# Key pages of a paged cache fetched by keys instead of by heads, in a hybrid decoder step

## The chip, the core and the metric

The kernel runs on one NeuronCore of a Trainium2 chip. Its time is the device time of one execution in microseconds (us). An execution was also taken by the hardware profiler; its trace has the start, length and waits of every instruction, the packets of the DMA engines, and the clock granted to TensorE. Engines are named PE (TensorE), PEld (TensorE's weight loads), DVE (VectorE), ACT (ScalarE), POOL (GpSimd) and SP (SyncE, which issues nearly all DMAs); SPq is SP's own queue of instructions. L724 is line 724 of the kernel.

## The reference, cut to what matters

One inference step of two layers over 256 prompt tokens and 64 sample tokens (8 sequences of 8), all in float32 with a width of 1024. The first layer is a retention layer. The second is block-sparse attention over shared keys and values. Its part that touches the change is the attention of the sample tokens over the paged cache:

```
def per_seq(args):                       # one of the 8 sequences
    q_s, kn, vn, pages = args            # pages: 2 numbers out of 20 physical pages
    k_past = cache_k[pages].reshape(past, MOBA_HEADS, MOBA_HD)      # 256 keys, 8 heads, 128
    v_past = cache_v[pages].reshape(past, MOBA_HEADS, MOBA_HD)
    k_s = concatenate([k_past, kn, zeros])
    v_s = concatenate([v_past, vn, zeros])
    return moba_attend(q_s, q_pos, k_s, v_s, rel_bias)
```

A page is 128 keys by 8 heads by 128 numbers, 512 KB, and lies in HBM key by key (a key's row of all heads is 4 KB). There are 16 pages of keys and 16 of values. `moba_attend` forms the scores of 8 queries against all keys for each head, a softmax with a bias, and the weighted sum of the values.

## The kernel before

All of the work is cut into 52 weight chunks of 1 MB (for each retention head one of q, one of k, two halves of v and two of the gate, then eight of `ro` and four each of `mq`, `mk`, `mv`, `mg`, `mo`). A chunk arrives in one of 3 buffers `w_raw`, ACT splits it into a rounded part `w_hi` (L1229), DVE forms the rest `w_lo` (L1569), each in four parts, into one of 2 buffers; PE then multiplies with `w_hi` and `w_lo` (L927, L930, and L911 for the stacked tile of sample tokens). PE waits for a part of `w_lo` before it uses it.

The order is a list of steps that `make_schedule` writes out by hand; every engine walks this list and does its share of each step, waiting on semaphores. Nothing is reordered at run time: a step that waits on an engine holds up all that stands behind it on that engine. Around the change these steps matter:

- `CHUNK c`: SP issues the load of chunk c + 2 (`load_chunk`, L682), after it has waited until DVE has formed the last parts of chunk c - 1. The chunks called W36 to W40 in the following are number 36 to 40: the four of `mk` (key weights, `in_w_kv`) and the first of `mv`.
- `ME 1` to `ME 6`: SP issues key pages 0 to 5 (`load_page`, L709 to L725).
- `KP n`: DVE waits for page n and turns it (a transpose of 32x32 blocks, L1860), into the layout in which PE's `KS` step multiplies 32 rows of it at a time (L1101). In the same step SP, for n from 1 to 10, issues key page n + 5, after it has waited until page n - 1 has been turned, for its buffer. For n from 13 on it issues value pages.
- `WS c k`: ACT and DVE split part k of chunk c. These stand between the `KP` steps in the same queues.

There are six slots for pages: four in `cache`, and two in the space of `mkT`, which is written later. So SP runs at most six key pages ahead of DVE. The semaphore of a slot counts 64 for a key page, 16 for each of its four DMAs, and `page_count` (L123) adds these up. The page number is read from `pages` into a register (L717) ahead of the DMAs. All of SP's DMAs go into one hardware queue, q1.

In the slot, partition 32 g + i holds keys i, 32 + i, 64 + i and 96 + i of the page, each with the 256 numbers of heads 2 g and 2 g + 1: four runs of 1 KB.

Of the kernel before, what the change touches and what calls it, by code (L numbers as in the profile page):

```python
# [111 lines left out]
def key_page(n):  # L112

    q, s, pg = n // 4, n % 4 // 2, n % 2
    return NPG * (4 * (q // 2) + 2 * s + q % 2) + pg


def page_slot(n):

    return n % NSLOT if n < 2 * NSLOT else (n - 2 * NSLOT) % NCP  # L120
# [191 lines left out]
def build(nc, a):  # L312
# [3 lines left out]
    with ctx:  # L316
# [247 lines left out]
        def page_at(n):  # L564

            at = page_slot(n)
            return cache[:, at, :] if at < NCP else early_pages[:, at - NCP, :]
# [66 lines left out]
        def chunk_source(c):  # L634
            kind, h, i = chunks[c]
            if kind in PAIRED:
                src, off = {"rv": (a["ret_w_in"][0], 2 * RH * DK), "mk": (a["w_kv"], 0), "mv": (a["w_kv"], D),
                            "mo": (a["moba_w_out"][0], 0)}[kind]
                return src.rearrange("(k p) n -> p k n", p=P)[:, KT // 2 * i:KT // 2 * i + KT // 2, off + 512 * h:off + 512 * h + 512]
            if kind[0] == "r" and kind != "ro":  # L640
                col = {"rq": h * DK, "rk": RH * DK + h * DK,
                       "rg": 2 * RH * DK + RH * DV + h * DV + i * 256}[kind]
                return a["ret_w_in"][0].rearrange("(k p) n -> p k n", p=P)[:, :, col:col + 256]
            if kind == "ro":
                return a["ret_w_out"][0].rearrange("(k p) n -> p k n", p=P)[:, KT * h:KT * h + KT, 256 * i:256 * i + 256]
            src, off = {"mq": (a["moba_w_in"][0], 0), "mg": (a["moba_w_in"][0], D)}[kind]
            return src.rearrange("(k p) n -> p k n", p=P)[:, :, off + 256 * h:off + 256 * h + 256]

        def chunk_view(buf, c, s):
            return buf[:, s, :].rearrange("p (k n) -> p k n", k=x_pieces(c))  # L650
# [16 lines left out]
        def _(sp):  # L667
# [41 lines left out]
            def load_page(n):  # L709

                m, vals = (n - 16, True) if n >= 16 else (key_page(n), False)
                before = n - (NCP if n >= 2 * NSLOT + NCP else NSLOT)
                if before >= 16:
                    sp.wait_ge(pv_done, before - 15)
                elif before >= 0:
                    sp.wait_ge(kt_done, before + 1)
                page = sp.value_load(pages[0:1, m:m + 1], min_val=0, max_val=a["cache_k"].shape[0] - 1)  # L717
                if vals:
                    sp.dma_start(page_at(n), a["cache_v"][bass.ds(page, 1)].rearrange("o p h d -> p (o h d)"))\
                        .then_inc(cache_loaded[page_slot(n)], 16)  # L720
                    return
                src = a["cache_k"][bass.ds(page, 1)].rearrange("o (c i) h d -> i (o c) (h d)", i=32)
                for g in range(4):
                    sp.dma_start(page_at(n)[32 * g:32 * g + 32, :].rearrange("p (c x) -> p c x", c=4), src[:, :, 256 * g:256 * g + 256])\  # L724
                        .then_inc(cache_loaded[page_slot(n)], 16)  # L725

            to, src = chunk_view(w_raw, 0, 0), chunk_source(0)
# [17 lines left out]
            for step in steps:  # L745
                kind = step[0]
                if kind == "CHUNK":
                    c = step[1]
# [17 lines left out]
                elif kind == "KT":  # L766
                    h = step[1]
# [7 lines left out]
                elif kind == "SC":  # L775
                    h = step[1]
# [12 lines left out]
                elif kind == "OP":  # L789
                    h = step[1]  # L790
# [23 lines left out]
                elif kind == "ME" and 1 <= step[1] <= NSLOT:  # L814
                    if step[1] == 1:
                        sp.wait_ge(pages_loaded, 16)
                        await_ret_over(sp)
                        sp.dma_start(knw[:, :], bass.AP(a["k_norm_w"].tensor, 0, [[0, P], [1, HD]])).then_inc(knw_loaded, 16)
                    load_page(step[1] - 1)
                elif kind == "KP":  # L820
                    n = step[1]
                    if 1 <= n <= 16 - NSLOT:
                        load_page(n + NSLOT - 1)
                    elif n >= 16 - NCP + 1:
                        load_page(n + NCP - 1)
                elif kind == "SE" and step[1] == 1:
                    await_ks(sp, 3)
                    sp.dma_start(tb[:, :, :], bass.AP(scratch.tensor, FAR - P, [[skew, P], [LINE, MH], [1, TP]]))\
                        .then_inc(tb_loaded, 16)
                elif kind == "KX" and step[1] % 2 == 0:  # L830
                    p = step[1] // 2
                    for n, t in enumerate(tile_order("mk", p, 1)):
                        m = TOK[t][1]
                        sp.wait_ge(rows_done, 3 * p + n + 1)
                        sp.dma_start(k_out[t][:, 512 * p:512 * p + 512], rows[0:m, t, :]).then_inc(rows_stored, 16)
                elif kind == "SN":
                    load_page(16 + NCP - 1)
                elif kind == "PV" and 1 <= step[1] <= 16 - NCP:
                    load_page(15 + NCP + step[1])
                elif kind == "YA" and step[1] == 0:  # L840
                    for t in range(3):
                        await_read(sp, *tile_use("mv", 3 + t))
                    for t, (c0, m) in enumerate(TOK):
                        store(v_out[t], mvp[:, t, :] if t < 2 else mvs[0:TS, :])
                elif kind == "TILE" and chunks[step[1]][0] == "mo":
                    p, t = chunks[step[1]][1], step[2]
                    await_read(sp, *tile_use("mo", 3 * p + t))
                    sp.dma_start(y_out[t][:, 512 * p:512 * p + 512], rows[0:TOK[t][1], t, :]).then_inc(rows_stored, 16)
# [1245 lines left out]
```

## Time and profile before

| | |
|---|---|
| three runs | 506.54, 506.27, 503.84 us; median 506.27 |
| the profiled execution | 503.63 us, of which its span (first to last instruction) is 501.6 us |
| PE busy | 490.5 us, 98% of the span |
| DVE, ACT, POOL busy | 357.9, 261.2 and 97.5 us |
| DMA | 125.54 MB in 86771 packets, 250 GB/s over the span |
| key pages: issues, size, median time to landing | 48 into `cache`, 128 KB, 5.7 us; 16 into `mkT`, 128 KB, 5.5 us |
| value pages | 16, 512 KB, 4.8 us |
| chunks of `in_w_kv` | 8, 1024 KB, 8.7 us |
| granted TensorE clock | 0.999 of full speed in the mean |

A row of a timeline gives the start in us from the start of the span, the length, the engine, the line, the operation, what it writes and reads, a count, and in brackets the idle time of the engine before it and what ended that. A row of stretches gives the length, for each engine its busy time with a count of instructions, the granted clock, the DMA share and the rate. The DMA share is the packets' time over 16 engines' time; it can exceed 1, since packets overlap on an engine. Of a DMA's packets those under 512 bytes in a stretch of large transfers are mostly the writes that report its completion.

### The profile page before, as it was taken

The numbers are of one execution on the slowest core, as the hardware profiler recorded it, in microseconds if no ns is written. First come the engines' busy times: TensorE is split into PE (matmuls) and PEld (weight loads), VectorE is DVE, ScalarE is ACT, GpSimd is POOL, SyncE is SP. The second block draws the span as 40 slices with busy tenths as digits, with TensorE's granted clock in tenths as the row PEclk, the third lists the DMA queues.
The fourth block names the chain that finished last, engine by engine and source line by source line (L and its number), as shares of the span: only waits on it lengthen the run. The fifth ranks groups of instructions, "written<-read, shape, count | busy, mean of one in ns | idle before, by whom it ended". The sixth has DMA issues, their size and how long they took to land.

```text
span 501.6 us, 9903 instructions
## 1 busy us (share of the span) xinstructions
PE 490.5 (98%) x3689; PEld 423.9 (85%) x3689; DVE 357.9 (71%) x633; ACT 261.2 (52%) x536; POOL 97.5 (19%) x139
## 2 busy tenths in 40 slices
PE   8999999999999999999999999999799999999997
PEld 6989978899778987799799999987567878999885
DVE  3955539884799819895589978996865764776662
ACT  6735532564427715366454455853637655655630
POOL 0291003620073200920000052454002000000000
PEclk9999999999999999999999999999999999999999
DMA  9993979999899898999936979979998567683211
GB/s 264 350 344 113 273 252 304 383 364 230 280 338 392 245 225 307 352 348 255 257 131 219 345 237 276 230 172 200 256 316 262 186 205 236 232 309 135 85 52 52
DMA packets 86771, 125.54 MB, mean 250 GB/s; under 512 B 5492, under 2 KB 51525, under 8 KB 86597
## 3 DMA queue, kind: packets, MB, share of 16 engines
q1 hardware_dynamic: 85874, 124.63, 80.7%
q8 instruction: 29, 0.48, 0.4%
q0 software_dynamic: 768, 0.28, 0.4%
q14 instruction: 18, 0.14, 0.1%
q10 hardware_dynamic: 82, 0.02, 0.0%
HBM read 98.93 MB, written 27.57 MB: 252 GB/s over the span
## 4 chain that ended last, share of the span: by engine, by line
PE 90%; DMA 3%; DVE 2%; ACT 2%; issue 2%; SPq 1%; POOL 0%; DVEq 0%; ACTq 0%; POOLq 0%
PE bank L930 46%; PE bank L927 17%; PE bank L911 7%; PE bank L1039 3%; DMA w_raw<-in_w_kv 2%; PE bank L1159 2%; PE bank L1053 1%; PE bank L986 1%; SPq L724 1%; PE bank L1205 1%; PE bank L1019 1%; PE bank L1021 1%; PE bank L1020 1%; PE bank L1007 1%; PE bank L1192 1%
## 5 line engine op out<-in xcount | busy, mean ns | idle before, releaser
L1569 DVE TENSOR_TENSOR w_lo<-w_raw,w_hi 128x512 fp32r<-128x512 f32 x207 | 143.2, 731 | 65.8 <-ACT w_hi L1229 65.0
L1229 ACT ACTIVATE w_hi<-w_raw 128x512 fp32r<-128x512 f32 x208 | 118.6, 620 | 71.6 <-PE bank L930 35.7
L930 PE MATMUL bank<-xn_hi,w_hi 128*128 128x320 f32 x320 | 100.2, 317 | 0.8 <-ACT w_hi L1229 0.7
L930 PE MATMUL bank<-xn_hi,w_lo 128*128 128x320 f32 x320 | 97.7, 309 | 0.1
L930 PE MATMUL bank<-xn_lo,w_hi 128*128 128x320 f32 x320 | 97.6, 309 | 0.0
L927 PE MATMUL bank<-w_hi,xn_hi 128*128 128x512 f32 x160 | 64.8, 405 | 0.0
L930 PEld LDWEIGHTS bank<-xn_hi,w_hi 128*128 128x128 f32 x320 | 59.7, 188 | 5.0 <-issue 2.9
L927 PE MATMUL bank<-w_lo,xn_hi 128*128 128x512 f32 x160 | 62.5, 391 | 0.0
L927 PE MATMUL bank<-w_hi,xn_lo 128*128 128x512 f32 x160 | 62.5, 390 | 0.0
L930 PE MATMUL bank<-ym_hi,w_hi 128*128 128x320 f32 x192 | 60.9, 317 | 0.0
L930 PEld LDWEIGHTS bank<-xn_lo,w_hi 128*128 128x128 f32 x320 | 59.8, 188 | 0.4 <-DVE xn_lo L1618 0.2
L930 PEld LDWEIGHTS bank<-xn_hi,w_lo 128*128 128x128 f32 x320 | 59.7, 188 | 0.3 <-DVE w_lo L1569 0.3
L930 PE MATMUL bank<-ym_hi,w_lo 128*128 128x320 f32 x192 | 59.3, 309 | 0.0
L930 PE MATMUL bank<-ym_lo,w_hi 128*128 128x320 f32 x192 | 59.3, 309 | 0.0
L1788 DVE SCALAR_TENSOR_TENSOR st<-st,bank 128x512 f32<-128x512 f32 x64 | 39.7, 684 | 5.2 <-PE bank L1053 5.2
L1997 POOL TENSOR_TENSOR fin<-raw_qk,cst 128x320 f32<-128x320 f32 x16 | 17.3, 1101 | 109.3 <-DMA out_ret_state_prompt<-fin 101.7
L930 PEld LDWEIGHTS bank<-ym_hi,w_hi 128*128 128x128 f32 x192 | 36.1, 188 | 1.8 <-issue 1.7
L927 PEld LDWEIGHTS bank<-w_hi,xn_hi 128*128 128x128 f32 x160 | 30.0, 188 | 8.6 <-issue 3.1
L930 PEld LDWEIGHTS bank<-ym_lo,w_hi 128*128 128x128 f32 x192 | 36.1, 188 | 0.1
L930 PEld LDWEIGHTS bank<-ym_hi,w_lo 128*128 128x128 f32 x192 | 36.0, 188 | 0.0
L927 PEld LDWEIGHTS bank<-w_lo,xn_hi 128*128 128x128 f32 x160 | 30.1, 188 | 6.6
L927 PEld LDWEIGHTS bank<-w_hi,xn_lo 128*128 128x128 f32 x160 | 30.1, 188 | 5.5
(289 smaller groups left out, 783.6 us busy)
## 6 DMA issues: line engine op xcount, KB each, us to landing
w_raw<-in_ret_w_in SPq DMA_DIRECT2D x23, 1024.0 KB, 11.3
st<-in_state_ret SPq DMA_DIRECT2D x32, 512.0 KB, 8.6
out_ret_state_sample<-st SPq DMA_DIRECT2D x32, 512.0 KB, 4.5
w_raw<-in_ret_w_out SPq DMA_DIRECT2D x8, 1024.0 KB, 8.5
w_raw<-in_moba_w_in SPq DMA_DIRECT2D x8, 1024.0 KB, 6.5
w_raw<-in_w_kv SPq DMA_DIRECT2D x8, 1024.0 KB, 8.7
cache<-in_cache_v SPq DMA_DIRECT2D x16, 512.0 KB, 4.8
cache<-in_cache_k SPq DMA_DIRECT2D x48, 128.0 KB, 5.7
```

The costliest lines, as they stand in the source:

```text
L724: sp.dma_start(page_at(n)[32 * g:32 * g + 32, :].rearrange("p (c x) -> p c x", c=4), src[:, :, 256 * g:256 * g + 256])\
L911: mm = pe.matmul(bank[b][:, :], xn_hi[:, k, TP:T + TS], w[:, wk, :], start=k == 0 and n == 0, stop=k == KT - 1 and n == 1)
L927: mm = pe.matmul(bank[b][0:m, :], x[:, k, c0:c0 + m], w[:, wk, :], **flags)
L930: mm = pe.matmul(bank[out][:, 0:T], w[:, wk, P * tile:P * tile + P], x[:, k, :], **flags)
L986: mm = pe.matmul(bank[5][0:m, col:col + n], kT[:, d, j:j + m], qT[:, d, i0:i0 + n], start=d == 0, stop=d == 1)
L1007: mm = pe.matmul(o[:, P:TP], vp[:, 1, at], sT_own[:, :], start=False, stop=True)
L1039: mm = pe.matmul(bank[5][32 * j:32 * j + 32, :], qz[:, q0:q0 + 32], st[:, b, DV * d:DV * d + DV], start=False, stop=g == 1 and d == 1, ski ...
L1159: mm = pe.matmul(bank[7][32 * j:32 * j + 32, P * u:P * u + P], window(8 * half_at + 4 * (j // 2) + 2 * pg + j % 2, b % 4), page_at(16 + m) ...
L1229: act.activation(w_hi[:, c % 2, part], w_raw[:, c % RAW, part], ACT.Copy).then_inc(w_hi_done, 1)
L1569: dve.tensor_tensor(w_lo[:, c % 2, part], w_raw[:, c % RAW, part], w_hi[:, c % 2, part].bitcast(F32), ALU.subtract).then_inc(w_lo_done, 1)
L1788: dve.scalar_tensor_tensor(state, state, math.exp(NEW * LOG_DECAY[h]), bank[up_bank(b, d)][:, :], ALU.mult, ALU.add).then_inc(bank_read[up ...
L1997: done(pool.tensor_tensor(to, x, tab, ALU.mult))
```

## The change

The key page is still fetched with four DMAs of 128 KB, of 128 runs of 1 KB each, and every run ends in the same place. Before, DMA g fetched heads 2 g and 2 g + 1 of all 128 keys into the 32 partitions from 32 g on. Now DMA c fetches keys 32 c to 32 c + 31 with all heads, into 1 KB of each of the 128 partitions.

```
-                src = a["cache_k"][bass.ds(page, 1)].rearrange("o (c i) h d -> i (o c) (h d)", i=32)
-                for g in range(4):
-                    sp.dma_start(page_at(n)[32 * g:32 * g + 32, :].rearrange("p (c x) -> p c x", c=4), src[:, :, 256 * g:256 * g + 256])\
+                src = a["cache_k"][bass.ds(page, 1)].rearrange("o (c i) h d -> (o c) i (h d)", i=32)
+                for c in range(4):
+                    sp.dma_start(page_at(n)[:, 256 * c:256 * c + 256], src[c].rearrange("i (g x) -> g i x", g=4))\
                         .then_inc(cache_loaded[page_slot(n)], 16)
```

The DMA's two sides, outermost first, as counts:

| | destination (SBUF) | source (HBM) |
|---|---|---|
| before | 32 partitions, 4 runs, 256 numbers | 32 keys (4 KB apart), 4 groups of keys (128 KB apart), 256 numbers |
| after | 128 partitions, 1 run, 256 numbers | 4 pairs of heads (1 KB apart), 32 keys (4 KB apart), 256 numbers |

On SP, around the load of W39 (the rows are the last two DMAs of page 12, the chunk, and the beginning of page 13; ISA rows set registers), before:

```order
L724 DMA cache<-in_cache_k 32x4x256
L724 ISA
L724 DMA cache<-in_cache_k 32x4x256
L682 DMA w_raw<-in_w_kv 128x4x512
L717 TENSOR_LOAD pages
L717 ISA x2
L724 ISA
L724 DMA cache<-in_cache_k 32x4x256
```

The same rows now:

```order
L724 DMA cache<-in_cache_k 128x1x256
L724 ISA
L724 DMA cache<-in_cache_k 128x1x256
L682 DMA w_raw<-in_w_kv 128x4x512
L717 TENSOR_LOAD pages
L717 ISA x2
L724 ISA
L724 DMA cache<-in_cache_k 128x1x256
```

No row has moved; only the shape of the destination differs, in all 64 DMAs of key pages. PE, DVE, ACT and POOL have the same rows as before.

## Rows read from the trace of the kernel before

**Rows 1.** The page's chain that ended last: shares of the span by engine.
```profile
PE 90%; DMA 3%; DVE 2%; ACT 2%; issue 2%; SPq 1%; POOL 0%; DVEq 0%; ACTq 0%; POOLq 0%
```

**Rows 2.** SP's timeline: start us, length us, line, transfer, how many.
```profile
301.71 4.47 SPq L724 DMA_DIRECT2D cache<-in_cache_k  x8
306.63 0.40 SPq L682 DMA_DIRECT2D w_raw<-in_w_kv  x1
...
316.25 0.40 SPq L682 DMA_DIRECT2D w_raw<-in_w_kv  x1
...
328.61 1.82 SPq L724 DMA_DIRECT2D cache<-in_cache_k  x4
330.53 0.40 SPq L682 DMA_DIRECT2D w_raw<-in_w_kv  x1
331.69 8.34 SPq L724 DMA_DIRECT2D cache<-in_cache_k  x12
340.81 5.28 SPq L724 DMA_DIRECT2D mkT<-in_cache_k  x8
346.86 2.18 SPq L724 DMA_DIRECT2D cache<-in_cache_k  x4
349.15 0.40 SPq L682 DMA_DIRECT2D w_raw<-in_w_kv  x1
350.31 8.33 SPq L724 DMA_DIRECT2D cache<-in_cache_k  x12
358.74 0.40 SPq L682 DMA_DIRECT2D w_raw<-in_w_kv  x1
```

**Rows 3.** Stretches, with TensorE's idle time; columns are named in the first row.
```profile
core 0: us, PE busy (x) PEld busy (x) DVE busy (x) ACT busy (x) POOL busy (x), PEclk, DMA share, GB/s
...
352.00:370.00 18.00, 13.52 (x177) 9.32 (x176) 14.54 (x23) 8.51 (x23) 0.00 (x0) 1.00 1.08 280
370.00:400.00 30.00, 29.33 (x312) 22.80 (x311) 19.65 (x43) 19.80 (x49) 2.88 (x5) 1.00 0.75 251
```

**Rows 4.** ACT's timeline, splits of W39 and W40; in brackets idle before.
```profile
360.74 1.67 ACT L1229 ACTIVATE w_hi<-w_raw 128x512 fp32r<-128x512 f32 x3 [1.61 <-DMA w_raw<-in_w_kv]
...
369.29 1.16 ACT L1229 ACTIVATE w_hi<-w_raw 128x512 fp32r<-128x512 f32 x2 [4.76 <-DMA w_raw<-in_w_kv]
372.21 0.59 ACT L1216 ACTIVATE rows<-bank 64x512 f32<-64x512 f32 x1 [1.77 <-PE bank L911]
```

**Rows 5.** DVE's timeline: turning of pages 6, 7 and 15.
```profile
339.01 1.25 DVE L1860 STREAM_TRANSPOSE mvp<-cache 128x1024 f32<-128x1024 f32 x1
343.24 1.25 DVE L1860 STREAM_TRANSPOSE mvp<-cache 128x1024 f32<-128x1024 f32 x1 [2.98 <-DMA cache<-in_cache_k]
...
367.20 1.23 DVE L1860 STREAM_TRANSPOSE mvp<-cache 128x1024 f32<-128x1024 f32 x1
```

**Rows 6.** Stretches, columns as in rows 3: v_rows, weights, key pages.
```profile
46.00:47.00 1.00, 1.00 (x9) 1.00 (x8) 0.00 (x0) 0.97 (x3) 0.23 (x1) 1.00 0.53 199
302.00:304.00 2.00, 2.00 (x16) 2.00 (x15) 1.84 (x5) 2.00 (x5) 0.28 (x1) 1.00 1.09 380
304.60:310.00 5.40, 5.40 (x39) 5.40 (x38) 5.37 (x8) 1.47 (x5) 0.00 (x0) 1.00 1.13 219
```

**Rows 7.** DMA packets from 302 to 304 us, then 304.6 to 310.
```profile
DMA packets 761, 0.76 MB, mean 380 GB/s; under 512 B 6, under 2 KB 761, under 8 KB 761
...
DMA packets 1147, 1.18 MB, mean 219 GB/s; under 512 B 123, under 2 KB 1025, under 8 KB 1146
```

**Rows 8.** DMA from 45 to 48.6 us, all v_rows; GB/s in 40 slices.
```profile
GB/s 0 0 0 137 68 114 68 137 91 68 159 182 205 182 205 182 228 182 182 205 228 228 182 182 137 137 137 182 159 205 228 205 182 159 250 182 137 68 46 0
DMA packets 288, 0.52 MB, mean 146 GB/s; under 512 B 32, under 2 KB 32, under 8 KB 288
```

**Rows 9.** SP's DMAs: ns min/median/max, first and last start.
```profile
L772 SPq DMA_DIRECT2D v_rows<-vs_split x16: 570/573/692, 44.0 to 223.7; - x16
...
L724 SPq DMA_DIRECT2D cache<-in_cache_k x48: 316/318/1445, 301.7 to 358.3; - x48
```

## The prediction

> **What bounds the kernel now.** I read the chain that ended last first: TensorE holds 90% of the span [rows 1], so a change pays or costs only where it makes TensorE wait. Then the key pages. SP fetches sixteen of them, each with four DMAs of 128 KB, between 301.7 and 358.7 us, with weight chunks W36 to W40 (the w_kv rows) in the same in-order queue [rows 2] (the eight DMAs of pages 2 and 3, and of 4 and 5, stand between these rows). In that stretch the DMA engines are the bound: from 352 to 370 us their busy share is 1.08, and TensorE is busy for 13.52 us of 18, so 4.48 us are missing there; in the 30 us behind it only 0.67 are [rows 3]. The ACT rows say who is late: the split of W39 waited 1.61 us and that of W40 4.76 us for the DMA [rows 4]. On VectorE the turning of page 7 waited 2.98 us for its page, and the last page is turned at 367.20 us [rows 5]. So pages and weight chunks compete for the same DMA engines, and TensorE feels it a little already.
>
> The same views price the traffic. Ahead of the pages the last weights for q (1 KB packets to 128 partitions) run at 380 GB/s. Behind them the pages of before (1 KB packets, 32 partitions each) run at only 219 GB/s, at a full share of 1.13 [rows 6]. Each of the 16 engines moves about 24 GB/s in the first case and 13.7 in the second. The packet size is no reason for it, since 302 to 304 us is nearly all 1 KB packets (761 under 2 KB, 0.76 MB) [rows 7]; the narrow destination is what differs.
>
> **The change, step by step.** On SP the same 64 DMAs stand in the same places; on the other engines nothing changes. Each still has 128 runs of 1 KB. What changes is the pair of shapes: 32 partitions on both sides before; now 128 partitions on the destination, but a source that says 4 groups of heads, then 32 keys, then 256 numbers. The outermost counts no longer agree: 128 and 4.
>
> (1) How many engines carry it. The trace has one kind of DMA with outermost counts that disagree: v_rows, 64 partitions on the one side, 8 on the other (8x8x512 in the code: sequences, tokens, values). Four of them move 0.52 MB in 256 packets, and beside these stand exactly 32 small completion packets: 8 for each DMA [rows 8]. For the key pages, 32 and 32, the small packets are 123 beside 1.17 MB, which is 9 DMAs: 13.8 each, 16 with the window's edges cut [rows 7]. In its steady part v_rows reaches a share of 0.53 [rows 6]. So a DMA of 8 and 64 used 8 engines, and I read a DMA of 4 and 128 as using 4. The Trainium skill ("DMA: Bandwidth & Descriptors", section on why a DMA increments its semaphore by 16) says it as a rule: the number of engines is the largest up to 16 that divides both sides' slowest size that isn't 1, and on SP's queue they are the lowest-numbered ones. By that rule it is 4, and always the same four; the completion packets of v_rows agree with the first half, and no row here shows the second. Without the skill it is an assumption of mine that every page goes to the same four; if they rotated, the load would be as even as before (in rival B).
>
> (2) What one page then takes. v_rows moved 199 GB/s on 8 engines, 25 each [rows 6]; in the full stretches an engine does 24. Bounds for an engine that takes keys: 13.7 GB/s (the page rows of before) and 28 (228 GB/s on 8, which v_rows' small slices reach again and again [rows 8]). I take 24, for each of the four now writes to partitions of its own, and the narrow destination shared by 16 engines is gone. A page is 512 KB, 131 KB for each of 4 engines: 5.46 us. A weight chunk still goes over all 16, 65.5 KB each: 2.73 us, and it lands only when its share on the four busy engines has.
>
> (3) The queue. The four engines are free at 304.6 us, when the traffic ahead of the pages ends [rows 6]. In SP's order they get pages 0, 1, W36, 2, 3, W37, 4, 5, 6, W38, 7 to 12, W39, 13 to 15, W40. One after the other:
> - page 6 is in at 304.6 + 7 x 5.46 + 2 x 2.73 = 348.3 (turned at 339.0 now);
> - page 7 at 304.6 + 8 x 5.46 + 3 x 2.73 = 356.5 (343.24 now);
> - W39 at 304.6 + 13 x 5.46 + 4 x 2.73 = 386.5 (split begins at 360.74 now);
> - page 15 at 304.6 + 16 x 5.46 + 4 x 2.73 = 402.9 (turned at 367.20 now);
> - W40 at 405.6 (split begins at 369.29 now).
> SP never starves them: it may run 6 pages ahead of VectorE, 33 us of work at this pace. VectorE waits at each page with the w_lo splits behind it, and TensorE waits for those; that is how late pages reach it.
>
> (4) The end. W40 is 405.6 - 369.3 = 36.3 us late, page 15 35.7. Everything behind them is as it was, but for the 1.77 us that ACT now waits for TensorE behind W40's first split [rows 4], which is gone when TensorE has been standing for long: 34.5. The 4.48 us that TensorE loses before 370 are inside this difference of two times already.
>
> (5) SP's issue. A v_rows DMA holds SP for 573 ns, a key DMA for 318 [rows 9]. If the unequal shapes are the cause, 0.25 us for each DMA and 1.0 for a page: SP then needs about 3 us a page against 5.46 on the engines. Cost 0; the queue on the four engines hides it. If that cover were gone (16 engines), it would be seen, see below.
>
> (6) TensorE's clock. It is granted in full (1.00) through 352 to 370 us [rows 3], with 4.48 us idle in several pieces. With gaps of up to 5 us at each page it may fall to half for a while. Inside the starved stretch this costs nothing; behind it a few matmuls at most. Between 0 and 4 us, I take 0.5.
>
> Sum: 34.5 + 0.5 = +35 on the profiled execution, 503.63 us, whose span is 501.6: 538.6. The median of the runs, 506.27, lies 2.64 above that execution, so I say 541.3.
>
> **Rivals.**
> - A, the other side: all 16 engines take part. Then the wide destination brings pages to the rate of rows to 128 partitions, 380 against 219 GB/s, 1.4 us a page in place of 2.4; W39 and W40 come in time, and TensorE gets back its 4.48 us between 352 and 370. 499.1 for the profiled execution, 501.8 in the runs. It decides if completion packets are 64 a page. For it: the rates [rows 6], and that the destination is 128 partitions. The Trainium skill ("SBUF — State Buffer", the section on the DMA port swizzle) has the same rule, that partitions 0 to 31 reach 8 of 16 ports; the ratio 219 to 380 is near it. Against it: the 8 packets of v_rows, whose 64 partitions did not help. Chance 0.06.
> - B: 16 engines, but SP pays 0.25 us more for each DMA. W39 is issued behind 24 key DMAs in a row, +6 us; W40 behind 36, +9, at 367.9; at 380 GB/s it lands 3.5 us later, 2 us behind now. Chance 0.04, 508. Here I put also 8 engines, or four that rotate, at 25 GB/s each: about the 219 of now. Another 0.05, 504 to 510.
> - C: the four engines disturb each other. Engines on partitions 0 to 31 and 32 to 63 walk in step, and if these share a port (the same section of the skill says that bit 5 of the partition doesn't change the port) both may fall to the 13.7 of the page rows. A page is then 9.6 us: 304.6 + 16 x 9.6 + 5 x 2.73 = 471.9, 102.6 us late, 606 for the profiled execution. With the engines partly out of step it ends between. v_rows, whose shares also lie 32 partitions apart, showed no such loss. Chance 0.13, from 560 to 610.
>
> **How the numbers follow.** Forecast 0.72, at 541. Its own range comes from the rate: 28 GB/s gives 304.6 + 16 x 4.68 + 5 x 2.34 = 391.2, +20 after the 1.77, 526; 20 GB/s gives 6.55 and 3.28, 425.8, +54.7, 561. The range should reach a little into C: 522 to 580. Left out are A and B and most of C, near 0.2. Within 0.5% of 506.27 (about what the runs can tell from no change) lies most of B: 0.05. Faster: A and a rest of B, 0.06. Slower 0.89.
>
> **What would show it.** Right: in the stretch from 305 to about 400 us a DMA share near 0.3 and 100 GB/s; 16 small packets to a page in place of 64; key DMAs without a landing time, as the v_rows have none, or with one of tens of us; long waits of VectorE at L1860 for the cache DMA; the splits of W39 and W40 waiting for DMA; TensorE with gaps in 340 to 405, and all as before behind it. Step 2 is wrong if the share is near 0.3 but the rate under 80 GB/s. Step 1 is wrong if the share stays at 1 or the small packets at 64. Step 4 is wrong if the stretch behind W40 is longer or shorter than the 132 us of now. Step 5 shows in the ns of L724's DMAs.

## The result, and the profile after

The changed kernel takes 555.8 us in the median of 4 runs, against 505.3 us before: a ratio of 1.0995, with a 95% interval of 1.095 to 1.104. It is 10% slower. The profiled execution took 556.13 us, of which its span is 554.1 us. Ratios here and below compare undisturbed executions alone; two of the twelve of experiment 9 were disturbed, and they stand in its median but not in its ratio.

The stretch of the key pages is where it went. First the stretches of the changed kernel, with the columns of [rows 3], in order of time: the last weights for q ahead of the pages, a stretch in which TensorE starves, a page stretch with nothing beside it, a stretch around the last pages, and all that comes behind the split of W40.

```profile
core 0: us, PE busy (x) PEld busy (x) DVE busy (x) ACT busy (x) POOL busy (x), PEclk, DMA share, GB/s
302.00:304.00 2.00, 2.00 (x16) 2.00 (x15) 1.83 (x6) 2.00 (x5) 0.44 (x2) 1.00 1.08 383
360.00:370.00 10.00, 2.38 (x81) 1.58 (x92) 2.42 (x3) 1.74 (x3) 0.00 (x0) 0.50 0.28 91
372.20:389.80 17.60, 8.53 (x29) 6.21 (x29) 8.36 (x12) 5.88 (x15) 0.00 (x0) 0.81 0.27 89
410.00:420.00 10.00, 6.04 (x68) 4.42 (x80) 3.06 (x3) 0.00 (x0) 0.00 (x0) 0.83 0.93 291
420.34:554.10 133.76, 124.34 (x1031) 105.50 (x1012) 79.71 (x182) 69.53 (x171) 2.73 (x5) 0.98 0.51 176
```

From 372.2 to 389.8 us the DMA engines are used to 0.27 of sixteen, which is 4.3 engines, and move 89 GB/s; in [rows 6] the pages of before had a share of 1.13 and 219 GB/s. The weights ahead of the pages run at 383 GB/s, as before. TensorE is busy for 2.38 us of 10 between 360 and 370 us, and for 6.04 between 410 and 420. Behind W40 the stretch is 133.8 us long, against 132.3 in [rows 3, 4] (501.6 - 369.3).

The packets of that page stretch, the counterpart of [rows 7]:

```profile
DMA packets 1568, 1.57 MB, mean 89 GB/s; under 512 B 48, under 2 KB 1566, under 8 KB 1566
```

1.57 MB are 12 DMAs of 128 KB, three pages, in 17.6 us: 5.87 us each. Beside them stand 48 completion packets, 4 for a DMA, where the pages of before had about 14 to 16 and v_rows 8 [rows 8]. Per engine it is 22.3 GB/s.

ACT's splits that wait for a chunk, VectorE's turning of the pages that answer to [rows 5], and the ns of SP's DMAs that answer to [rows 9]:

```profile
337.96 1.15 ACT L1229 ACTIVATE w_hi<-w_raw 128x512 fp32r<-128x512 f32 x2 [8.46 <-DMA w_raw<-in_w_kv]
...
360.51 1.15 ACT L1229 ACTIVATE w_hi<-w_raw 128x512 fp32r<-128x512 f32 x2 [15.27 <-DMA w_raw<-in_w_kv]
...
399.27 1.67 ACT L1229 ACTIVATE w_hi<-w_raw 128x512 fp32r<-128x512 f32 x3 [5.52 <-DMA w_raw<-in_w_kv]
...
420.34 1.15 ACT L1229 ACTIVATE w_hi<-w_raw 128x512 fp32r<-128x512 f32 x2 [16.77 <-DMA w_raw<-in_w_kv]
```

```profile
343.78 1.25 DVE L1860 STREAM_TRANSPOSE tb<-mkT 128x1024 f32<-128x1024 f32 x1 [1.01 <-DMA mkT<-in_cache_k]
350.15 1.25 DVE L1860 STREAM_TRANSPOSE tb<-mkT 128x1024 f32<-128x1024 f32 x1 [4.55 <-DMA mkT<-in_cache_k]
...
366.32 1.25 DVE L1860 STREAM_TRANSPOSE mvp<-cache 128x1024 f32<-128x1024 f32 x1 [7.35 <-DMA cache<-in_cache_k]
...
372.19 1.25 DVE L1860 STREAM_TRANSPOSE ktc<-cache 128x1024 f32<-128x1024 f32 x1 [3.46 <-DMA cache<-in_cache_k]
...
378.07 1.25 DVE L1860 STREAM_TRANSPOSE ktc<-cache 128x1024 f32<-128x1024 f32 x1 [1.10 <-DMA cache<-in_cache_k]
...
389.81 1.25 DVE L1860 STREAM_TRANSPOSE scr<-mkT 128x1024 f32<-128x1024 f32 x1 [4.06 <-DMA mkT<-in_cache_k]
...
410.82 1.25 DVE L1860 STREAM_TRANSPOSE mvp<-cache 128x1024 f32<-128x1024 f32 x1 [4.06 <-DMA cache<-in_cache_k]
417.77 1.25 DVE L1860 STREAM_TRANSPOSE mvp<-cache 128x1024 f32<-128x1024 f32 x1 [5.13 <-DMA cache<-in_cache_k]
```

```profile
L724 SPq DMA_DIRECT2D cache<-in_cache_k x48: 537/1204/2236, 301.9 to 408.1; - x48
```

The splits are those of W37, W38, W39 and W40; the pages are 4, 5, 7, 8, 9, 11, 14 and 15. W39 is split 38.5 us later than in [rows 4] (399.27 against 360.74), W40 51.05 us later; page 7 is turned at 366.32 in place of 343.24, the last page at 417.77 in place of 367.20. Pages 7, 8 and 9 come 5.87 us apart, and page 11 twice that behind page 9. A key DMA holds SP for 1204 ns in the median, where it was 318.

### The profile page after: what moved, and what is told of

Its sections match the earlier page's. It is cut to its first block, busy times and chain, and to the rows that moved or that the text cites. A ratio compares the mean times of both kernels' runs of the same rounds, so it can differ in the third digit from the quotient of the medians.

```text
span 554.1 us, 9903 instructions
## 1 busy us (share of the span) xinstructions
PE 502.1 (91%) x3689; PEld 431.0 (78%) x3689; DVE 358.7 (65%) x633; ACT 260.8 (47%) x536; POOL 97.1 (18%) x139
## 4 chain that ended last, share of the span: by engine, by line
PE 74%; SPq 12%; DVE 5%; issue 4%; DMA 3%; ACT 2%; POOL 0%; DVEq 0%; ACTq 0%; POOLq 0%
PE bank L930 36%; PE bank L927 15%; SPq L724 9%; PE bank L911 5%; PE bank L1039 3%; SPq L717 2%; DVE w_lo L1569 2%; PE bank L1159 1%; DMA out_k_prompt<-rows 1%; PE bank L1053 1%; PE bank L986 1%; DMA cache<-in_cache_k 1%; PE bank L1205 1%; SPq L682 1%; ACT w_hi L1229 1%
## 5 line engine op out<-in xcount | busy, mean ns | idle before, releaser
L927 PE MATMUL bank<-w_hi,xn_hi 128*128 128x512 f32 x160 | 67.4, 421 | 3.9 <-DVE small L1737 2.0
L927 PE MATMUL bank<-w_lo,xn_hi 128*128 128x512 f32 x160 | 64.6, 404 | 0.0
L927 PE MATMUL bank<-w_hi,xn_lo 128*128 128x512 f32 x160 | 64.5, 403 | 0.0
L911 PE MATMUL bank<-w_hi,xn_hi 128*128 128x512 f32 x80 | 33.8, 423 | 11.7 <-DVE w_lo L1569 10.6
L927 PEld LDWEIGHTS bank<-w_hi,xn_hi 128*128 128x128 f32 x160 | 31.4, 196 | 14.3 <-issue 3.6
L927 PEld LDWEIGHTS bank<-w_lo,xn_hi 128*128 128x128 f32 x160 | 31.3, 196 | 7.2
L927 PEld LDWEIGHTS bank<-w_hi,xn_lo 128*128 128x128 f32 x160 | 31.5, 197 | 5.9
```

The costliest lines, as they stand in the source:

```text
L911: mm = pe.matmul(bank[b][:, :], xn_hi[:, k, TP:T + TS], w[:, wk, :], start=k == 0 and n == 0, stop=k == KT - 1 and n == 1)
L927: mm = pe.matmul(bank[b][0:m, :], x[:, k, c0:c0 + m], w[:, wk, :], **flags)
```

## The experiments

The kernel before was run again beside each; its medians lay between 505.6 and 506.4 us.

**1. Is it the number of engines, or the pieces of 1 KB to 128 partitions?** The same four DMAs, with a source that also counts 128 outermost:

```
-                src = a["cache_k"][bass.ds(page, 1)].rearrange("o (c i) h d -> (o c) i (h d)", i=32)
+                src = a["cache_k"][bass.ds(page, 1)].rearrange("o p h d -> p (o h d)")
-                    sp.dma_start(page_at(n)[:, 256 * c:256 * c + 256], src[c].rearrange("i (g x) -> g i x", g=4))\
+                    sp.dma_start(page_at(n)[:, 256 * c:256 * c + 256], src[:, 256 * c:256 * c + 256])\
```

> The changed kernel's four DMAs a page, 1 KB pieces to all 128 partitions, but read from rows of the page as they lie, so that both sides count 128 outermost (a partition then holds another key and other heads than it should; the sum of work is the same). Theory (the outermost counts 4 and 128 put a page on four engines): 64 completion packets a page, a page in under 2 us, a rate above 330 GB/s, no wait for W39 and W40, 498 to 503 us. Rival (pieces of 1 KB to 128 partitions are slow whatever the source): share and rate as in the changed kernel, about 556 us.

Measured: 501.3 us, ratio to before 0.990 (0.987 to 0.994). The stretches of this kernel that answer to [rows 3, 6], and the packets from 304.6 to 310 us:

```profile
304.60:310.00 5.40, 5.40 (x39) 5.40 (x39) 5.29 (x8) 1.47 (x5) 0.00 (x0) 1.00 0.90 272
312.00:317.00 5.00, 5.00 (x36) 5.00 (x35) 4.78 (x11) 3.73 (x9) 2.18 (x6) 1.00 0.51 161
352.00:370.00 18.00, 16.07 (x191) 12.01 (x190) 14.27 (x21) 8.43 (x21) 0.00 (x0) 1.00 0.91 305
...
DMA packets 1268, 1.47 MB, mean 272 GB/s; under 512 B 119, under 2 KB 988, under 8 KB 1267
```

The whole loss is gone, and 1% is gained on before. Of the 988 packets under 2 KB 119 are small, which leaves 869 of 1 KB, 6.8 key DMAs; the rest are 2 KB packets of W36. 119 small ones beside 6.8 key DMAs and a part of W36 fit 16 for each DMA, and not 4. The rate was below what I expected (272 GB/s, then 161 and 305). With a share of 0.51 from 312 to 317 us the engines are waiting for work, as SP's rows show:

```profile
307.70 5.74 SPq L724 DMA_DIRECT2D cache<-in_cache_k  x8
316.16 0.40 SPq L682 DMA_DIRECT2D w_raw<-in_w_kv  x1
```

Eight DMAs, 1.05 MB, take SP 5.74 us, which is 183 GB/s, and then it issues nothing for 2.7 us, until W37's buffer is free. ACT still waits 4.07 us for W40, which I had expected to be gone. So the destination and the size of the pieces are innocent; what costs is that the two sides' outermost counts differ. This source also reads 1 KB of each key, where the changed kernel reads 32 keys as they lie one behind the other. Nor is that the cause: the value pages are read as they lie too, with 128 partitions against 128 keys, and their 512 KB landed 4.8 us after the issue in the kernel before, less than the 5.87 us that four engines need for as much.

**2. Two engines in place of four.** Everything lands where it should (and `page_count` adds 128 for a key page in place of 64):

```
-                for c in range(4):
-                    sp.dma_start(page_at(n)[:, 256 * c:256 * c + 256], src[c].rearrange("i (g x) -> g i x", g=4))\
+                for half in range(2):
+                    for c in range(4):
+                        sp.dma_start(page_at(n)[64 * half:64 * half + 64, 256 * c:256 * c + 256],
+                                     src[c][:, 512 * half:512 * half + 512].rearrange("i (g x) -> g i x", g=2))\
```

> A page in eight DMAs of 64 KB, each to 64 partitions from 2 pairs of heads x 32 keys: outermost counts 2 and 64, everything lands where it should. Theory (engines = what divides both counts, here 2): 2 completion packets a DMA, share near 0.14, 45 GB/s, a page 262144/22.3 GB/s = 11.75 us; W40 at 304.6 + 16 x 11.75 + 5 x 4.4 = 514.6 in place of 420.3, about 650 us. Rival (SP's 1.2 us for each such DMA is the cost): 8 x 1.3 = 10.4 us a page only if SP is slow by itself, 628; rival (any unequal shape costs the same): 556.

Measured: 648.3 us, ratio 1.280 (1.271 to 1.289). A stretch of pages alone, and its packets:

```profile
430.00:450.00 20.00, 1.11 (x3) 0.33 (x1) 4.25 (x6) 2.63 (x8) 0.00 (x0) 0.50 0.14 45
...
DMA packets 886, 0.89 MB, mean 45 GB/s; under 512 B 27, under 2 KB 884, under 8 KB 884
```

Share 0.14, 45 GB/s, and 27 small packets beside 0.88 MB, which is 13.5 DMAs of 64 KB: 2 each. W40's split begins at 514.11 us where the queue of pages gave 514.6. The time follows the count of engines: 16, 4 and 2 give about 501, 556 and 648 us.

**3. Is SP's longer issue the bound?** One DMA a page, still 4 against 128, with the keys permuted (`page_count` adds 16):

```
-                src = a["cache_k"][bass.ds(page, 1)].rearrange("o (c i) h d -> (o c) i (h d)", i=32)
-                for c in range(4):
-                    sp.dma_start(page_at(n)[:, 256 * c:256 * c + 256], src[c].rearrange("i (g x) -> g i x", g=4))\
+                src = a["cache_k"][bass.ds(page, 1)].rearrange("o (i g) h d -> (o g) i (h d)", g=4)
+                sp.dma_start(page_at(n), src)\
```

> One DMA of 512 KB a page, outermost counts 4 and 128, runs of 4 KB (keys 4 i + g in the place of 32 g + i, so the keys are permuted). Theory (four engines are the bound, and SP's 1.2 us a DMA is only that it is held back by them): a page still takes 5.4 to 5.9 us, 548 to 557 us. Rival (SP's issue of 1.2 us a DMA is the bound, 4 to a page): a page 1.3 us of SP, 505 to 515 us.

Measured: 551.0 us, ratio 1.087 (1.080 to 1.093). A quarter of the DMAs saves 5 us of 50. The page's DMA now holds SP for up to 6.2 us:

```profile
L723 SPq DMA_DIRECT2D cache<-in_cache_k x12: 628/2758/6244, 303.2 to 389.2; - x12
```

So SP is held back by work already queued on the engines, and most of its time for an issue is a result. The changed kernel says the same by itself: its first six key DMAs take SP 0.54 to 0.73 us, near the 0.57 of v_rows, and the next two 1.06 and 2.07. In experiment 1, with equal counts, the median is 0.33. Runs of 4 KB go at 102 GB/s on four engines (the pages turned at 364.32 and 369.42 us are 5.1 us apart), runs of 1 KB at 89.

**4. Only the first six pages in the new form.**

```
+                if n < 6:
+                    (the changed kernel's four DMAs)
+                    return
                 (the four DMAs of the kernel before)
```

> Key pages 0 to 5 in the new form, 6 to 15 in the form of before. Theory (one queue on four engines, to be worked off in order): page 5 is in at 304.6 + 6 x 5.87 + 2 x 4.4 = 348.6 against 337.6 when it is turned in the kernel before, then pages at 2.4 us each catch up nothing: W40 some 12 us later than 369.3, 514 to 518 us. Rival (every page costs its 50/16 us): 524. Rival (the first six are fetched far ahead, so they are hidden): 505 to 508.

Measured: 528.5 us, ratio 1.043 (1.036 to 1.050). All three expectations missed: 514 to 518, 524 and 505 to 508. It is no case of "fetched ahead, therefore hidden": six pages of sixteen cost 23 us of the 50.

```profile
345.48 1.25 DVE L1866 STREAM_TRANSPOSE tb<-mkT 128x1024 f32<-128x1024 f32 x1 [1.00 <-DMA mkT<-in_cache_k]
355.30 1.25 DVE L1866 STREAM_TRANSPOSE tb<-mkT 128x1024 f32<-128x1024 f32 x1 [8.00 <-DMA mkT<-in_cache_k]
...
364.33 1.15 ACT L1235 ACTIVATE w_hi<-w_raw 128x512 fp32r<-128x512 f32 x2 [18.05 <-DMA w_raw<-in_w_kv]
...
393.55 1.15 ACT L1235 ACTIVATE w_hi<-w_raw 128x512 fp32r<-128x512 f32 x2 [5.72 <-DMA w_raw<-in_w_kv]
```

W40's split begins at 393.55, 24.3 us late, where I had 12. The 12 was a wrong comparison: I set page 5's arrival, 348.6, against 337.6, when the kernel before turns that page. It had been in its slot for 11 us by then; its DMAs there were issued by 321.5 us and landed within 5.2:

```profile
L724 SPq DMA_DIRECT2D mkT<-in_cache_k x8: 316/317/325, 317.4 to 321.5; - x8
...
DMA to landing us min/median/max: 4.8/5.0/5.2
```

In the kernel before the queue behind page 5 goes on at 328.61 [rows 2]; by my sum it does so at 348.6 here, 20.0 us later, which gives 505.7 + 20 = 525.7 against the 528.5 measured. Of the other 4.3 us of W40's delay the rows tell where they begin: page 5 is turned at 355.30, 6.7 us later than the 348.6, and 9.82 us behind page 4, where it was 6.37 in the changed kernel (343.78 and 350.15). Up to page 5 the queue on the four engines is the same in both. What differs is the twelve others, which here have pages 6 and later and W38 to fetch: the DMA share in that interval is 0.98, against 0.39. So the four carried page 5 at 13.3 GB/s each while the twelve were busy. By what the twelve slow them isn't shown.

**5. Is it the order in the queue or the bytes on the four engines?** W36 to W40 issued by ACT, on a queue of its own:

```
+                elif kind == "CHUNK" and 36 <= step[1] + 2 <= 40:
+                    c = step[1] + 2
+                    await_lo(act, c - RAW, 2)
+                    await_lo(act, c - RAW, 3)
+                    act.dma_start(chunk_view(w_raw, c, c % RAW), chunk_source(c)).then_inc(w_loaded[c % RAW], 16)
```

> The changed kernel with the loads of W36 to W40 issued by ACT, at the same step, on its own queue. Theory (the bytes of pages and chunks on the four engines set the pace, whatever the order): W39 and W40 come earlier, page 15 is still turned near 415 to 418 us, 550 to 556 us. Rival (the chunks are late because they stand behind the pages in one queue, and that is what costs): W40's split near 375, 510 to 525 us.

Measured: 555.7 us, ratio 1.099 (1.091 to 1.106), the same as the changed kernel. ACT waits for W36 2.60 us, for W37 2.02 and for W40 4.41, and for W38 and W39 not at all; the changed kernel waited 8.46 us for W37, 15.27 for W38, 5.52 for W39 and 16.77 for W40. The last page is turned at 420.61, 2.6 us behind the 415 to 418 that I expected, and about when W40 was split in the changed kernel (420.34). So the chunks come sooner and the pages later, and the time is the same: the order is of no account here, the bytes are.

**6. What a chunk costs on the four engines.** Only a quarter of each of W36 to W40 is fetched (the rest of the buffer keeps what lay there):

```
+                if 36 <= c <= 40:
+                    to, src = to[:, 0:1], src[:, 0:1]
                 sp.dma_start(to, src).then_inc(w_loaded[c % RAW], 16)
```

> The changed kernel, but of W36 to W40 only a quarter is fetched (256 KB each), the rest of these buffers is what lay there. Theory (on the four busy engines a chunk costs its own bytes and slows the pages while the other twelve fetch theirs, 4.4 us in all): each chunk 1.1 us or a little more, W40's split near 404 to 407, 539 to 543 us. Rival (the pages alone set the pace and the chunks fit beside them): 553 to 556.

Measured: 541.3 us, ratio 1.069 (1.063 to 1.074). W40's split begins at 405.26:

```profile
405.26 1.15 ACT L1231 ACTIVATE w_hi<-w_raw 128x512 fp32r<-128x512 f32 x2 [14.79 <-DMA w_raw<-in_w_kv]
```

15.1 us for three quarters of five chunks is 4.0 us for a whole one, if the cost goes by the bytes.

**7. The order of the partitions in the kernel before.** One edit in it, `for g in range(4)` to `for g in (0, 2, 1, 3)`:

> The kernel before, with its four DMAs of a page issued in the order of partitions 0, 64, 32, 96. Theory (the 219 GB/s of before come from a destination that reaches only a part of SBUF's entries, and partitions 0 to 63 share theirs): engines that have drifted apart by one DMA now write into different halves, the rate behind 304.6 us rises above 250 GB/s, up to 4 us gained, 501 to 504. Rival (16 engines work on one DMA at a time in step, so the order is of no account): 219 GB/s and 505.3 us, within 0.3%.

Measured: 504.3 us in 12 runs, ratio 0.994 (0.991 to 0.998). From 304.6 to 310 us the rate is 246 GB/s against 219 [rows 6] at the same share of 1.14, just short of the 250 I asked for, and in the profiled execution, the fastest of the twelve, TensorE is busy for 15.57 us of the 18 between 352 and 370 us, against 13.52 [rows 3]. The rate speaks against the rival (219 GB/s, the order of no account); the time alone, with an interval that reaches 0.998, would hardly do so. Of the kernels that neither leave out nor permute anything, this is the fastest, 0.6% under the kernel before and 9% under the changed one.

**8 to 10. Chunks issued earlier, to gain the rest.** From chunk 36 on (37 in the third), `load_chunk(c + 3)` in place of `load_chunk(c + 2)`, in the old order and in the order of 7:

```
-                    load_chunk(c + 2)
+                    if c < 36:
+                        load_chunk(c + 2)
+                    elif c == 36:
+                        load_chunk(c + 2)
+                        load_chunk(c + 3)
+                    else:
+                        load_chunk(c + 3)
```

> The kernel before, with the loads of W39 and of every chunk behind it issued one chunk earlier in SP's order (W39 ahead of pages 7 to 12, W40 ahead of pages 13 to 15); their buffers have been read by then. Theory (in the kernel before TensorE's 4.48 us between 352 and 370 are lost because W39 and W40 stand behind pages in the queue): ACT's waits for w_kv of 1.61 and 4.76 us go, pages come up to 3 us later, 500 to 503. Rival (the pages take the place as the bound): 505 to 507.

> Both edits: early chunks, and a page's DMAs in the order of partitions 0, 64, 32, 96. Theory: the order takes part of the pages' time away, so what the early chunks cost the pages is small: 498.5 to 502, no wait of ACT for w_kv, at most 1 us of VectorE for a page. Rival (one gain contains the other): as the better of the two alone, 501 to 503.

> The order 0, 64, 32, 96 and only W40 (and what is behind it) issued one chunk earlier, ahead of pages 13 to 15; W39 stays behind page 12. Theory: page 7 doesn't wait, ACT's 4.6 us for W40 go, pages 13 to 15 have slack; 500 to 503, under the 504.3 of the order alone. Rival (pages 13 to 15 come late in its place): 504 to 507.

Measured: 508.1 us (1.004, 1.001 to 1.007), 505.7 us (0.997, 0.994 to 1.000) and 506.1 us (0.999, 0.997 to 1.002). All three missed what I expected of them (500 to 503, 498.5 to 502 and 500 to 503), and none beats experiment 7. The first has lost ACT's waits for W39 and W40, as expected, and VectorE waits for page 7 in their place:

```profile
347.30 1.25 DVE L1866 STREAM_TRANSPOSE mvp<-cache 128x1024 f32<-128x1024 f32 x1 [6.71 <-DMA cache<-in_cache_k]
```

That is 6.71 us where [rows 5] have 2.98. In the second, ACT doesn't wait for a chunk either, and VectorE waits 2.11 us for page 7 and 1.05 for page 8. In the third, VectorE waits 4.00 us for page 13, and ACT still 1.41 for W40. Where the DMA engines are full, a chunk that goes ahead pushes a page back: that is the rival of the first and the third experiment. Its time holds in the third (504 to 507); the first came out above it (505 to 507), and the second above both of its expectations (the rival had 501 to 503).

## Why the prediction was right in its mechanism and 14.5 us short

The forecast was 541.3 us and slower, from four engines in one queue; measured are 555.8. The range, 522 to 580, held it. For the profiled executions it is 538.6 against 556.1, 17.5 us apart; the runs are 3.0 closer, since I carried over the 2.64 us by which the runs of before lay above their profile, and the profile of after lies 0.34 above its runs.

- **Step 1, the number of engines: right.** 4 completion packets a DMA and a share of 0.27. That it is the same four for each page, which no row had shown, follows from that share: in the page stretch several DMAs are under way and it never rises. Experiments 1 and 2 show the cause by itself. Which four they are no row shows. The rule of the Trainium skill ("DMA: Bandwidth & Descriptors", the section on why a DMA increments its semaphore by 16) holds here for 2, 4 and 8 by the completion packets (27, 48 and 32 of them in the stretches read).
- **Step 2, the time of a page: mis-sized.** 5.87 us in place of 5.46, or 22.3 GB/s for an engine in place of 24. Over 16 pages 6.6 us. Experiment 3 brings it to 25.5 with runs of 4 KB, so the length of the runs has a part in it; why 1 KB runs went at 24 over sixteen engines [rows 6] and at 22.3 over four stays open.
- **Step 3, the time of a chunk on the four engines: mis-sized, the largest term.** From 304.6 to W40's split at 420.3 are 115.7 us; 16 pages of 5.87 leave 21.8 for five chunks, 4.36 each, in place of 2.73: 8.1 us. Experiment 6, built for this term, gives 4.0. A chunk's own bytes at 22.3 GB/s are 2.9. The rest lies in the bursts, in which the twelve other engines are busy too. From 312 to 319 us, around W36, the changed kernel moved this:

```profile
312.00:319.00 7.00, 7.00 (x50) 7.00 (x49) 6.57 (x15) 5.31 (x14) 3.16 (x9) 1.00 0.75 188
...
DMA packets 874, 1.31 MB, mean 188 GB/s; under 512 B 25, under 2 KB 440, under 8 KB 874
```

1.31 MB in 7 us, of which 0.79 MB is the twelve other engines' share of W36; the four moved 0.52 MB, 18.7 GB/s each, below their 22.3. Two places with no chunk between two pages say the same: page 15 comes 6.95 us behind page 14 (410.82 and 417.77), with a DMA share of 0.96 from 410.8 to 417.8 us, and in experiment 4 page 5 comes 9.82 us behind page 4 with a share of 0.98. That is 18.9 and 13.3 GB/s for each of the four. No run was built to test this by itself, and the cause behind it stays open.
- **Step 4, the end: wrong by 1.8 us.** I let the 1.77 us of ACT's wait behind W40's first split vanish. It stayed, as 1.75, with another releaser: the copy at L1216 overwrites `rows`, and in the code it has to wait until the keys' output has been stored, by DMAs that stand in the same queue behind page 15, W40 and a value page. The chain, the time to landing of the last two of these DMAs, and ACT's row:

```profile
413.81 7.68 DMA out_k_prompt<-rows
421.49 1.75 issue
...
DMA to landing us min/median/max: 6.5/7.9/9.4
...
423.24 0.59 ACT L1216 ACTIVATE rows<-bank 64x512 f32<-64x512 f32 x1 [1.75 <-issue]
```

The chain counts the 1.75 us as "issue". But 413.81 + 9.4 is 423.2 us, when the copy begins, and so I read them as the wait for this DMA.
- **Step 5, SP's issue: right that it costs nothing, wrong in its size.** 1204 ns in the median and not 573. The unequal counts raise it from 0.32 or 0.33 us to the 0.54 to 0.73 of the first six DMAs; the rest is the work queued on the engines (experiment 3).
- **Step 6, the clock: between its bounds.** The split of chunk 41 is 51.03 us later than before (435.35 against 384.32), the last split of that chunk 52.28 (440.32 against 388.04), and the first of the next 52.49 (444.23 against 391.74). From 434 to 442 us the granted clock is 0.84 and 0.73, behind stretches such as 410 to 420 us, where TensorE was busy for 6.04 us of 10:

```profile
434.00:438.00 4.00, 2.50 (x12) 2.13 (x13) 2.03 (x4) 3.48 (x9) 0.00 (x0) 0.84 0.28 86
438.00:442.00 4.00, 4.00 (x77) 3.20 (x75) 0.69 (x1) 2.31 (x4) 0.00 (x0) 0.73 0.98 376
...
437.02 0.63 PE L927 MATMUL bank<-w_hi,xn_hi 128*128 128x512 f32 x1
```

The matmuls at L927 take 0.63 us there, and 0.39 at the full clock. The span grew by 52.5 us and W40's split by 51.05, so 1.45 us come behind it, where I took 0.5. With it the four terms, 6.6, 8.1, 1.8 and 0.95, make up the 17.5. In experiment 2 the granted clock is 0.50, the lower level of 1.2 GHz, through the whole stretch shown, and costs nothing, for TensorE is waiting.

Of the rivals, A is what experiment 1 built, the same pieces over 16 engines: I gave 501.8 and it was 501.3. That it came so near is in part luck. A let the pages go at 380 GB/s, W40 come in time and TensorE get back all of its 4.48 us between 352 and 370; the rates were 272, 161 and 305, ACT still waited 4.07 us for W40, and TensorE was busy for 16.07 of the 18 us, so it got back 2.55. C, four engines that halve each other's pace, did not happen: 22.3 GB/s and not 13.7. B is out by the share.

## What to carry to other kernels

Read the two outermost counts of a DMA against each other before its destination. If one of them is small and the other isn't (8 against 64, 4 against 128, 2 against 64 here), only as many engines carry it, and everything behind it in the queue that needs all engines comes as late as they do: here a change that moved the same bytes in the same 64 transfers cost 50 us. Completion packets in a stretch, divided by the DMAs of that kind in it, tell the number of engines from a trace in one row. And where the engines are full, earlier weights are paid with later pages.

## What the runs showed of the hardware that I had not expected

- SP's time for an issue is not a property of the transfer alone: with counts of 4 and 128 it is 0.54 to 0.73 us for the first six DMAs, 1.2 us in the median of all with pieces of 1 KB, and up to 6.2 us for one DMA of 512 KB.
- Destinations of 32 partitions run at 219 GB/s one after the other, and at 246 when neighbours in the queue lie in different halves of the 128 partitions; nothing but their order differs.
- Four engines that are behind lose more pace while the twelve others are busy: 22.3 GB/s each when alone, 18.9 beside full transfers behind page 14, and 13.3 in experiment 4.
- A transfer that is fetched well ahead of its use isn't free for that: page 5 had 11 us to spare, but six pages on four engines put off all that stands behind them in the queue by 20 us and more.
- An engine that reads 4 KB runs moves 25.5 GB/s, one that reads 1 KB runs 22.3, on four engines.
